# Gate sums in the softmax, fewer and other products of zeros, and stages that open with the high part, in a two-block model on one core

## The reference, cut to what matters

```python
blocks = kv[:, idx] + pe[:, None, :]
return jax.nn.gelu(flat @ w1) @ w2
```

```python
z = rmsnorm(x, norm_mix) @ w_in
q_a = partial_rope(rmsnorm(q_a, att_q_norm), cos, sin)   # k_a the same
scores = einsum(q, k) * hd ** -0.5                        # softmax with sinks, then probs @ v
log_f = jax.nn.log_sigmoid(f_pre)                         # mLSTM gates, four heads
b = jnp.cumsum(log_f, axis=-1)
m_t = jnp.maximum(log_inter, jnp.max(log_d, axis=-1))
u = jax.nn.relu(rmsnorm(x, norm_ffn) @ w_ff1)
return x + (u * u) @ w_ff2
```

## Time and profile before

| | us |
|---|---|
| median of three runs | 2673.26 |
| lowest and highest of them | 2667.30, 2674.91 |
| the profiled execution | 2667.08 |
| its span, first to last instruction | 2665.4 |
| TensorE busy | 2571.5 |
| VectorE busy | 1797.8 |
| ScalarE busy | 1208.2 |
| GpSimd busy | 998.0 |

### The profile page before, as it was taken

How to read it: one execution, slowest core, us unless ns; L and a number is a source line. 1 busy time by engine, 2 the same in 40 slices (tenths; PEclk the granted TensorE clock), 3 DMA queues, 4 the chain that set the end, 5 groups by cost and what they waited for, 6 DMA issues and landing times.

```text
span 2665.4 us, 51124 instructions
## 1 busy us (share of the span) xinstructions
PE 2571.5 (96%) x19552; PEld 2420.5 (91%) x19552; DVE 1797.8 (67%) x2822; ACT 1208.2 (45%) x2019; POOL 998.0 (37%) x588
## 2 busy tenths in 40 slices
PE   3999999999999999999999999999999999999999
PEld 3999999888889989989998878999888999988999
DVE  6775898467686577559984666765853576753676
ACT  2444456245554454444552554444552344652444
POOL 2433986200033233358870000333650244650244
PEclk9999999799999999999999999999999999999999
DMA  8775774233477567767643335775434566433464
GB/s 329 250 271 174 264 228 149 88 102 96 142 252 261 174 229 271 248 216 234 198 130 92 103 96 179 274 243 166 132 115 124 152 186 188 147 122 123 152 188 134
DMA packets 131491, 481.28 MB, mean 181 GB/s; under 512 B 14848, under 2 KB 14848, under 8 KB 130560
## 3 DMA queue, kind: packets, MB, share of 16 engines
q1 hardware_dynamic: 107280, 389.12, 46.1%
q0 software_dynamic: 23040, 83.90, 8.6%
q10 hardware_dynamic: 1008, 6.00, 0.6%
HBM read 475.82 MB, written 3.15 MB: 180 GB/s over the span
## 4 chain that ended last, share of the span: by engine, by line
PE 86%; DVE 6%; POOL 3%; ACT 3%; issue 1%; DVEq 1%; DMA 0%; SPq 0%; ACTq 0%; POOLq 0%
PE ps L451 22%; PE ps L453 21%; PE ps L452 21%; PE ps L693 4%; PE ps L2324 2%; PE ps L543 2%; PE ps L2291 2%; POOL ring_parts L1963 1%; POOL eb L2015 1%; PE ps L491 1%; PE ps L920 1%; DVE ring_parts L1433 1%; DVE eb L1381 1%; PE ps L903 1%; PE ps L793 1%
## 5 line engine op out<-in xcount | busy, mean ns | idle before, releaser
L452 PE MATMUL ps<-u_parts,high 128*128 128x256 f32 x3840 | 1087.9, 283 | 0.0
L452 PEld LDWEIGHTS ps<-u_parts,high 128*128 128x128 f32 x3840 | 737.7, 192 | 0.4
L1054 ACT ACTIVATE high<-ring 128x1024 fp32r<-128x1024 f32 x461 | 485.7, 1056 | 395.2 <-PE ps L453 367.7
L451 PE MATMUL ps<-ac_parts,high 128*128 128x256 f32 x1920 | 550.4, 287 | 18.5 <-DVE u_parts L1455 10.0
L453 PE MATMUL ps<-ac_parts,ring_parts 128*128 128x256 f32 x1920 | 545.5, 284 | 0.0
L1968 POOL TENSOR_TENSOR ring_parts<-ring,high 128x1024 fp32r<-128x1024 f32 x88 | 224.9, 2555 | 473.8 <-ACT high L1054 473.8
L451 PE MATMUL ps<-h_parts,high 128*128 128x256 f32 x1360 | 393.7, 289 | 4.5 <-POOL ring_parts L1963 3.6
L451 PEld LDWEIGHTS ps<-ac_parts,high 128*128 128x128 f32 x1920 | 365.9, 191 | 25.1 <-issue 15.9
L453 PE MATMUL ps<-h_parts,ring_parts 128*128 128x256 f32 x1360 | 386.0, 284 | 0.0
L1963 POOL TENSOR_TENSOR ring_parts<-ring,high 128x1024 fp32r<-128x1024 f32 x138 | 331.3, 2407 | 105.0 <-ACT high L1054 103.7
L453 PEld LDWEIGHTS ps<-ac_parts,ring_parts 128*128 128x128 f32 x1920 | 364.2, 190 | 0.0
(11 more groups left out here) (448 smaller groups left out, 4820.5 us busy)
## 6 DMA issues: line engine op xcount, KB each, us to landing
ring<-stream_dram SPq DMA_DIRECT2D x736, 512.0 KB, 3.7
xc<-ada_dram POOLq DMA_DIRECT2D x84, 512.0 KB, 5.8
z<-ada_dram POOLq DMA_DIRECT2D x36, 512.0 KB, 6.7
qr<-ada_dram POOLq DMA_DIRECT2D x36, 512.0 KB, 6.5
h_aside<-ac ACTq DMA_DIRECT2D x2, 1024.0 KB, 4.4
eb<-ada_dram POOLq DMA_DIRECT2D x4, 512.0 KB, 5.2
h<-h_aside ACTq DMA_DIRECT2D x2, 1024.0 KB, 6.0
conb<-con_dram ACTq DMA_DIRECT2D x1, 1032.0 KB, 7.7
```

Source lines behind the costliest of these rows:

```text
L451: mm(out, hi, xh, start=start, stop=False, **kw)
L452: mm(out, hi, xl, start=False, stop=False, **kw)
L1054: act(high_of(m, i), chunk_of(m, i), ACT.Copy).then_inc(made, 1)
```

## The change

It has four parts. A new function orders the products of an opening pair otherwise: at each tile it waits for the high part of the input and makes the four products with it, then waits for the low part and makes the remaining two. It is used in all openings; the FFN of block two now opens with a pair too, followed by `down(0)` and then `up(2)`, `down(1)`, and so on.

```diff
+def pair_by_tiles(t, mm, m, outs, chunks, xh, xl, high, low):
+    for k in range(ND):
+        a, b = k * P, (k + 1) * P
+        high(k)
+        for out, i in zip(outs, chunks):
+            mm(out, high_of(m, i)[:, a:b], xh[:, k], start=k == 0, stop=False, skip_group_check=True)
+            mm(out, low_of(m, i)[:, a:b], xh[:, k], start=False, stop=False, skip_group_check=True)
+        low(k)
+        ends = [mm(out, high_of(m, i)[:, a:b], xl[:, k], start=False, stop=k == ND - 1, skip_group_check=True)
+                for out, i in zip(outs, chunks)]
+    return ends
...
-                for k in range(ND):
-                    t.wait_ge(sem["ulo"], at("ulo", 28 * q + k + 1))
-                    for c in range(2):
-                        last = product3(mm, ps[:, 4 + 2 * c, c * S:(c + 1) * S], m, i + c, k, m.uhi_ffn[:, k], m.ulo[:, k],
-                                        start=k == 0, stop=k == ND - 1, skip_group_check=True)
-                        if k == ND - 1:
-                            last.then_inc(done, 1)
+                ends = pair_by_tiles(t, mm, m, [ps[:, 4 + 2 * c, c * S:(c + 1) * S] for c in range(2)], (i, i + 1),
+                                     m.uhi_ffn, m.ulo, lambda k: t.wait_ge(sem["uhi"], at("uhi", 28 * q + k + 1)),
+                                     lambda k: t.wait_ge(sem["ulo"], at("ulo", 28 * q + k + 1)))
+                ends[0].then_inc(done, 1)
+                ends[1].then_inc(done, 1)
...
-        t.wait_ge(sem["lo"], at("lo", 1))
-        for k in range(ND):
-            t.wait_ge(sem["ulo"], at("ulo", 8 + k + 1))
-            last = product3(mm, ps[:, 4, 0:S], m, E_FFN, k, m.uhi_ffn[:, k], m.ulo[:, k],
-                            start=k == 0, stop=k == ND - 1)
-        last.then_inc(done, 1)
+        t.wait_ge(sem["lo"], at("lo", 2))
+        ends = pair_by_tiles(t, mm, m, [ps[:, 4 + c, 0:S] for c in range(2)], (E_FFN, E_FFN + 1), m.uhi_ffn, m.ulo,
+                             lambda k: t.wait_ge(sem["uhi"], at("uhi", 8 + k + 1)),
+                             lambda k: t.wait_ge(sem["ulo"], at("ulo", 8 + k + 1)))
+        ends[0].then_inc(done, 1)
+        ends[1].then_inc(done, 1)
+        down(E_FFN + 2, 0, 0)
         with t.Fori(0, 3) as it:
             for q in range(9):
-                up(E_FFN + 1 + 2 * q, 1 + q, 9 * it + 1 + q)
-                down(E_FFN + 2 + 2 * q, q, 9 * it + q)
+                up(E_FFN + 3 + 2 * q, 2 + q, 9 * it + 2 + q)
+                down(E_FFN + 4 + 2 * q, 1 + q, 9 * it + 1 + q)
```

```diff
         for b in range(2):
+            if b == 0:
+                for _ in range(8):
+                    mm(ps[:, unit(j), :], m.zero[:, 0:P], m.zero[:], start=True, stop=True)
             t.wait_ge(sem["kpe"], at("kpe", b + 1))
...
-            products_of_zeros(mm, m, (11, 8)[k])
+            products_of_zeros(mm, m, (14, 10)[k])
...
-        t.wait_ge(sem["copied"], at("copied", 10))
-        products_of_zeros(mm, m, 12)
         for n in range(5):
```

```diff
+        t.wait_ge(sem["oc"], at("oc", 1))
+        t.wait_ge(sem["mt"], at("mt", 1))
+        for a in range(2):
+            last = mm(ps[:, 0, 4 * a:4 * a + 4], m.ow[:, 3, a * P:(a + 1) * P],
+                      m.con[0:4, CON["ident"]:CON["ident"] + 4], start=True, stop=True)
+        last.then_inc(sem["rt"], 1)
         scale_side(0)
...
+        t.wait_ge(sem["mtc"], at("mtc", 1))
         head_out(0)
...
+        def gate_sums():
+            nc.vector.tensor_tensor_scan(w(2), w(7), w(1), 0.0, ALU.mult, ALU.add)
+            v.drain()
+            tt(w(3), w(0), w(2), ALU.subtract)
+            v.drain()
+            nc.vector.tensor_tensor_scan(w(4), w(3), w(3), 0.0, ALU.max, ALU.max)
+            v.drain()
+            ts(w(5), w(4), -1.0, None, ALU.mult)
+            v.drain()
+            tt(w(6), w(5), w(2), ALU.subtract).then_inc(sem["mt"], 1)
...
         for i in range(4):
             weights(i)
             if i + 2 < 4:
                 maxima(i + 2)
+            if i == 1:
+                gate_sums()
+        v.wait_ge(sem["rt"], at("rt", 1))
+        nc.vector.tensor_copy(m.rt, ps[:, 0, 0:8].rearrange("p (a h) -> p a h", a=2)).then_inc(sem["mtc"], 1)
+        v.drain()
```

More of the change, by code:

```diff
@@ L617, in layer @@
                 low_made(C_GLU + 1)
-                for k in range(ND):
-                    t.wait_ge(sem["ulo"], at("ulo", 8 + k + 1))
[L620 to L623, removed]
-                            last.then_inc(done, 1)
+                ends = pair_by_tiles(t, mm, m, [ps[:, unit(3 * c), c * S:(c + 1) * S] for c in range(2)], (C_GLU, C_GLU + 1),
+                                     m.uhi, m.ulo, lambda k: t.wait_ge(sem["uhi"], at("uhi", 8 + k + 1)),
+                                     lambda k: t.wait_ge(sem["ulo"], at("ulo", 8 + k + 1)))
+                ends[0].then_inc(done, 1)
+                ends[1].then_inc(done, 1)
             else:
@@ L2085, in layer @@
         t.wait_ge(sem["lo_g"], at("lo_g", E_Q + 2))
[L2086 to L2092, removed]
+        ends = pair_by_tiles(t, mm, m, [ps[:, unit(3 * c), c * S:(c + 1) * S] for c in range(2)], (E_Q, E_Q + 1),
+                             m.uhi2, m.ulo, lambda k: t.wait_ge(sem["uhi"], at("uhi", k + 1)),
+                             lambda k: t.wait_ge(sem["ulo"], at("ulo", k + 1)))
+        ends[0].then_inc(done, 1)
+        ends[1].then_inc(done, 1)
         j += 1
@@ L2164, in layer @@
         j += 1
[L2165 to L2169, removed]
         t.wait_ge(sem["copied"], at("copied", 11))
@@ L2210, in layer @@
         t.wait_ge(sem["dupc"], at("dupc", 1))
-        t.wait_ge(sem["mtc"], at("mtc", 1))
         scores(0)
@@ L2350, in down @@
             x.then_inc(done, 1)
-        t.wait_ge(sem["lo"], at("lo", 1))
-        for k in range(ND):
-            t.wait_ge(sem["ulo"], at("ulo", 8 + k + 1))
-            last = product3(mm, ps[:, 4, 0:S], m, E_FFN, k, m.uhi_ffn[:, k], m.ulo[:, k],
-                            start=k == 0, stop=k == ND - 1)
-        last.then_inc(done, 1)
+        t.wait_ge(sem["lo"], at("lo", 2))
+        ends = pair_by_tiles(t, mm, m, [ps[:, 4 + c, 0:S] for c in range(2)], (E_FFN, E_FFN + 1), m.uhi_ffn, m.ulo,
+                             lambda k: t.wait_ge(sem["uhi"], at("uhi", 8 + k + 1)),
+                             lambda k: t.wait_ge(sem["ulo"], at("ulo", 8 + k + 1)))
+        ends[0].then_inc(done, 1)
+        ends[1].then_inc(done, 1)
+        down(E_FFN + 2, 0, 0)
         with t.Fori(0, 3) as it:
             for q in range(9):
-                up(E_FFN + 1 + 2 * q, 1 + q, 9 * it + 1 + q)
-                down(E_FFN + 2 + 2 * q, q, 9 * it + q)
-        for f in range(28, NF2):
+                up(E_FFN + 3 + 2 * q, 2 + q, 9 * it + 2 + q)
+                down(E_FFN + 4 + 2 * q, 1 + q, 9 * it + 1 + q)
+        for f in range(29, NF2):
             up(E_FFN + 2 * f - 1, f, f)
@@ L2627, in layer @@
         v.drain()
-        nc.vector.tensor_tensor_scan(w(2), w(7), w(1), 0.0, ALU.mult, ALU.add)
-        v.drain()
-        tt(w(3), w(0), w(2), ALU.subtract)
-        v.drain()
-        nc.vector.tensor_tensor_scan(w(4), w(3), w(3), 0.0, ALU.max, ALU.max)
-        v.drain()
-        ts(w(5), w(4), -1.0, None, ALU.mult)
-        v.drain()
-        tt(w(6), w(5), w(2), ALU.subtract).then_inc(sem["mt"], 1)
         for n in range(5):
@@ L2653, in layer @@
             tt(dst, dst, m.tmp[n % 2], ALU.add).then_inc(sem["rope"], 1)
-        v.wait_ge(sem["rt"], at("rt", 1))
-        nc.vector.tensor_copy(m.rt, ps[:, bank(21), 0:8].rearrange("p (a h) -> p a h", a=2))\
-            .then_inc(sem["mtc"], 1)
+        def gate_sums():
[8 more added lines that the diff above has]
+            tt(w(6), w(5), w(2), ALU.subtract).then_inc(sem["mt"], 1)
         def maxima(i):
```

## The result

Over 20 runs each the changed kernel took 2673.7 us in the median (2667.3 to 2684.0), the kernel before 2667.2 (2660.9 to 2674.9). The ratio is 1.0022, with a 95% interval of 1.0013 to 1.0031: a little slower and clear of the noise, where 2659 us was forecast. The means are 2674.7 against 2667.8, +6.9 us with a standard error of 1.4. A second series gave 1.0032 (1.0017 to 1.0048), +8.2 us. The forecast was set on the median of three runs, 2673.26 us, which happened to lie 6 us above the median of twenty: the change was to take 14 us off and added 7, a miss of 21 us.

The account below looks back on a forecast made before the run. TensorE, busy 96% of the span, was taken to bound the kernel. Terms -9.8 -5.2 -2.6 -2.5 -1.8 +4.6 +3.4 = -13.9 us, set on the median of 2673.26, gave 2659 us; 8-in-10 range 2647 to 2672.

Parts of the forecast that it names:

- zeros ahead of the rotations out: Block two: twelve products of zeros ahead of the rotations cover no wait; removing them saves 2.6 us a layer, -5.2.
- zeros at the compression products: Block one: eight zeros fill TensorE's 2.13 us idle time and the clock's fall goes: -9.8 us for two layers.
- openings of block one and of the projections: High part first ends pairs two products behind the last low part: -2.6 us in block one, -2.5 in block two's projections.
- opening of block two's FFN: Both chunks opened together, down product earlier despite a new 2.3 us hole: -1.8 us; clock falls behind the holes priced separately.
- gate sums: Block two's softmax: five moved VectorE operations delay tile three's weights, transposes wait 2.3 us a layer: +4.6 us.
- The bounds of this term, -5.2 and -1.8: Rotation zeros out: -5.2 us for two layers, or -1.8 if a short clock fall (1.7 us) comes in each layer.
- The first rival: Low clock at the compression products stays despite the eight zeros: -4.1 us in all, 2669 us; chance 0.20.
- half a fall of the short kind: Behind four new holes (transposes, FFN, two layers), half get a 3.4 us half-speed stretch costing 1.7 us each: +3.4.

Follow-up runs that it names:

- the kernel without the compression zeros: Changed kernel with twelve rotation zeros, gate sums and one-chunk FFN opening put back, eight compression zeros removed: 1.0001, +0.4 ± 1.1 us against the kernel before.
- the gate chunk first: Changed kernel with gate sums and FFN opening put back, no rotation zeros, third gate chunk ahead of the duplicating product: 0.9967 of the kernel before, -7.7 ± 1.3 us.

## Why the prediction was wrong

The whole was forecast at -13.9 us and measured at +6.9 and +8.2. All terms in us, each measured alone against the kernel before; predicted falls of the clock are added to the part that they belong to.

| part | predicted | measured |
|---|---|---|
| zeros ahead of the rotations out | -5.2 | +9.5 ± 1.5 |
| zeros at the compression products | -9.8 | -4.2 ± 1.9 |
| openings of block one and of the projections | -5.1 | +0.4 ± 1.1 |
| opening of block two's FFN | -1.8 + 1.7 | -1.0 ± 1.2 |
| gate sums | +4.6 + 1.7 | +3.3 ± 1.6 |
| sum | -13.9 | +8.0 ± 3.3 |

The measured terms make up the change within their errors. (The openings' term is from the kernel without the compression zeros; the gate sums' small product stands at its new place in it.)

*The step that failed* is "So they cover no wait: 12 x 0.216 = 2.6 us come off in each layer ... What is late next is rotation five, which waits for VectorE's first sum as before." That they covered no wait for the queries was true; rotation five's wait of 0.5 us even went with them. What they covered lies behind: the rotary operations' place among GpSimd's subtractions. The zeros held them back until the subtraction of 1938.31 was nearly over, and the next came 5.64 us behind its end. Taken out, the second query's product falls behind the subtraction of 1928.82 and loses 1.85 us; by that delay the last query's sum and the key's sum meet the next two. The bounds of this term, -5.2 and -1.8, held no block at all, though the same kind of block was priced a few paragraphs on for the gate sums, from the earlier trace rows. Two thirds of the miss of 21 us are this term: 14.7, of which 7.7 are the waits (-5.2 became +2.5) and 7 the lower clock, for which the bound had 3.4.

The rule drawn on there, of the Trainium skill ("SBUF — State Buffer", section "SBUF: two separate sides"), is borne out in both places: a VectorE operation with two SBUF inputs that starts early within a GpSimd subtraction ends 0.3 us behind it (0.42 becomes 2.09 to 2.60 us), while the multiplication with one input in PSUM (L2653, at 1928.87 within the subtraction of 1928.82) keeps its 0.42. It would have told of this term too, had the operations behind a moved start been laid against GpSimd's.

*Compression products.* The zeros hide in the idle time, and the wait is 0.4 to 0.5 us, as forecast. What failed is "so it was the gap and not the narrow products that went with the fall": a fall comes in 22 of 26 layers though the gap is gone, and the gain is 4 to 5 us, not 9.8. The first rival was the nearer to the truth, but took the gain to be nothing.

*Openings.* Block one's waits at its four openings went from 10.0 to 7.9 us, but the low part of a chunk, next in the row, waits 1.4 us longer: of 2.6 us, comparing the starts of the same products in the two profiles leaves some 1.5. Over all profiles, five with the old and thirteen with the new opening, the time from the zeros to the 61st product behind them is 0.5 to 0.6 us shorter in the first FFN of each layer (0.46 was forecast an opening) and only 0.1 in the second. In the projections the mechanism held: with the new opening no profile, of thirteen, had low clock in it; with the old one four of five had, in the first layer. By these, some 3 us should show in the runs; they show +0.4 ± 1.1. What takes them back was not found.

*FFN and gate sums.* Both waits came as written. The hole before the first down product, which had none in the earlier trace rows, is 2.16 us (forecast 2.3). The third tile's transposes, which did not wait in the earlier trace rows, wait 1.96 us here and 1.97 in the second layer (2.3 forecast); four scalings of 0.87 us in all take 2.88 beside the subtraction:

```profile
1969.38 0.68 DVE L2661 TENSOR_TENSOR_SCAN kv<-kv 4x256 f32<-4x256 f32 x1
...
1972.38 2.37 POOL L2830 TENSOR_TENSOR ring_parts<-ring,high 128x1024 fp32r<-128x1024 f32 x1 [3.44 <-ACT high L2396]
...
1972.55 2.88 DVE L2699 TENSOR_SCALAR eb<-eb,small 128x128 f32<-128x128 f32 x4
...
1975.48 0.66 PE L2194 MATMUL ps<-con,eb 128*128 128x128 f32 x4 [1.96 <-DVE eb L2699]
```

No scan took over 0.7 us. The clock behind these holes was sized wrong, half a fall of the short kind for each. A fall follows the FFN's hole in 6 of 14 layers that have it, but one stands at this place in 8 of 22 layers with the old opening too, so hardly any of it is new. Behind the third tile's transposes one came in 1 of 14.

## What to carry to other kernels

Before taking dead work out, ask not only which wait it covers but what starts earlier behind it and what that meets: lay each VectorE operation that moves against GpSimd's operations. The better cure is a wait that keeps the two engines apart, on the side whose result is not wanted yet (GpSimd's here), not filler on the engine that bounds. And waiting can cost more than its length, through the clock: six zeros with 2.6 us of wait were 6 us slower than twelve without. It need not: with the gate chunk first, waits of 1.5 and 0.7 us a layer stood where the zeros had been, and the mean clock kept its level.

## What the runs showed of the hardware

Every stretch of low clock (1.2 in the place of 2.4 GHz) in the 18 profiles that ends inside the kernel lasts 3.4, 6.8 or 10.2 us to within 0.1. The mean clock differs from run to run of one program and goes with most of its spread: 0.001 more of it is some 2.6 us less of time.

VectorE and GpSimd: a product or sum of two tiles of 128x256 in SBUF takes 0.41 to 0.43 us on VectorE alone and 2.09 to 2.60 us when it starts early within GpSimd's subtraction of 128x1024 (2.35 to 2.4 us), which keeps its own time.

The same loop of block two's FFN runs at one of two paces at full clock: 345 or 341 products are recorded in 40 us, a difference of 2 us over the stage. It differs between the two layers of one profile and between programs with the same loop. The changed kernel, second layer, and the one with the old opening back, first and second layer (TensorE alone):

```profile
2520.00:2560.00 40.00, 40.00 (x341) 1.00 0.64 186
```

```profile
2110.00:2150.00 40.00, 40.00 (x341) 1.00 0.62 184
...
2520.00:2560.00 40.00, 40.00 (x345) 1.00 0.64 192
```

The changed kernel, profiled twice, had the same pace in the same layer both times. What sets it is open.
